# Expert stage of a transformer block: the three experts whose weights are loaded ahead become steps 0, 1 and 2, in place of steps 0, 2 and 4

## The reference, cut to what matters

```
p_grp = softmax(h @ wg + bg)            # 4 groups, the best one is taken
p_in  = softmax(le[token, grp])         # 8 experts in a group, the best 2 are taken
eidx  = grp * 8 + e_in                  # two experts per token
for each expert, over the rows (tokens) that chose it:
    hb = silu(xb @ w1[e]) * (xb @ w3[e])        # 1024 -> 512, twice
    y  = (hb @ w2[e]) * gate                     # 512 -> 1024
```

## Time and profile before

| | us |
|---|---|
| median of 3 runs | 1504.38 |
| the profiled execution | 1504.77 |
| its span | 1502.9 |
| TensorE busy in the span | 1333.3 (89%) |
| mean GB/s over the span | 214 |

### The profile page before, as it was taken

How to read it: one execution, slowest core, us unless ns; L and a number is a source line. 1 busy time by engine, 2 the same in 40 slices (tenths; PEclk the granted TensorE clock), 3 DMA queues, 4 the chain that set the end, 5 groups by cost and what they waited for, 6 DMA issues and landing times.

```text
span 1502.9 us, 17013 instructions
## 1 busy us (share of the span) xinstructions
PE 1333.3 (89%) x6325; PEld 672.8 (45%) x6325; DVE 596.4 (40%) x1331; ACT 396.5 (26%) x878; POOL 82.2 (5%) x113
## 2 busy tenths in 40 slices
PE   4899999999997889998899973999999999989940
PEld 3644444464665445544455541454344444434420
DVE  3526447510335766665522246232222322312216
ACT  4234311113666565554422220000000000000005
POOL 0000000010002100000000000000000000000014
PEclk9999999999998999999999985999999999999985
DMA  9712145330004692000092262899999999999979
GB/s 339 173 42 101 67 168 173 107 113 0 1 1 113 116 323 85 1 1 1 18 376 96 98 256 102 339 391 391 404 399 401 406 403 395 392 412 396 408 266 297
DMA packets 111534, 322.01 MB, mean 214 GB/s; under 512 B 28876, under 2 KB 53592, under 8 KB 103128
## 3 DMA queue, kind: packets, MB, share of 16 engines
q1 hardware_dynamic: 98376, 290.96, 52.5%
q0 software_dynamic: 6288, 18.90, 4.0%
q10 hardware_dynamic: 6784, 11.02, 2.0%
HBM read 280.44 MB, written 43.03 MB: 215 GB/s over the span
## 4 chain that ended last, share of the span: by engine, by line
PE 38%; DMA 8%; SPq 5%; DVE 4%; issue 2%; ACT 2%; POOL 1%; ACTq 0%; DVEq 0%; POOLq 0%
PE ps L1495 7%; PE ps L1550 7%; DMA arena<-expert_w 7%; PE ps L1539 7%; PE ps L1589 6%; SPq L675 4%; PE ps L1399 2%; PE ps L1416 2%; PE ps L1436 2%; PE ps L1529 1%; ACT arena L1064 1%; POOL arena L866 1%; PE ps L1470 1%; DMA arena<-d_y,arena 1%; SPq L673 1%
## 5 line engine op out<-in xcount | busy, mean ns | idle before, releaser
L1249 PE MATMUL ps<-arena 128*128 128x512 f32 x512 | 222.0, 593 | 0.0
L1550 PE MATMUL ps<-arena 128*32 128x256 f32 (+1 forms) x1408 | 189.7, 484 | 15.2 <-DMA arena<-expert_w 13.3
L1589 PE MATMUL ps<-arena 128*32 128x256 f32 (+2 forms) x832 | 152.7, 498 | 3.5 <-issue 2.2
L1249 PEld LDWEIGHTS ps<-arena 128*128 128x128 f32 x512 | 96.6, 190 | 117.8 <-issue 117.6
L1260 PE MATMUL ps<-arena 128*128 128x512 f32 (+1 forms) x384 | 144.5, 534 | 1.4 <-DVE arena L1685 1.4
L1550 PEld LDWEIGHTS ps<-arena 128*32 128x32 f32 (+1 forms) x1408 | 71.7, 123 | 118.8 <-issue 101.7
L1539 PE MATMUL ps<-arena 128*128 128x512 f32 x256 | 114.3, 604 | 2.8 <-DVE arena L2111 2.8
L1495 PE MATMUL ps<-arena 128*128 128x512 f32 x256 | 114.4, 599 | 0.0
L1064 ACT ACTIVATE arena<-arena 128x640 f32<-128x640 f32 (+7 forms) x128 | 92.7, 726 | 59.1 <-DVE arena L1899 59.1
L1260 PEld LDWEIGHTS ps<-arena 128*128 128x128 f32 x384 | 72.8, 192 | 66.2 <-issue 57.3
L1416 PE MATMUL ps<-arena 128*128 128x128 f32 x528 | 80.3, 286 | 24.2 <-ACT arena L1064 12.1
(11 more groups left out here) (339 smaller groups left out, 1267.7 us busy)
## 6 DMA issues: line engine op xcount, KB each, us to landing
arena<-expert_w SPq DMA_DIRECT2D x96, 2048.0 KB, 34.0
arena<-ada_w SPq DMA_DIRECT2D x12, 2048.0 KB, 9.3
d_y<-arena SPq DMA_DIRECT2D x25, 512.0 KB, 6.6
arena<-x SPq DMA_DIRECT2D x16, 512.0 KB, 5.2
arena<-w_in SPq DMA_DIRECT2D x4, 2048.0 KB, 10.8
d_y<-arena ACTq DMA_DIRECT2D x40, 128.0 KB, 7.9
arena<-w_out SPq DMA_DIRECT2D x2, 2048.0 KB, 14.1
out<-arena SPq DMA_DIRECT2D x8, 512.0 KB, 2.6
```

Source lines behind the costliest of these rows:

```text
L1249: last = nc.tensor.matmul(b, w(k), hT[:, k, 512 * c:512 * c + 512], start=(k == 0), stop=(k == KT - 1))
L1550: last = nc.tensor.matmul(ps[width * j:width * j + width, 2 if width == 64 else 3, 0:span], xgT[s][:, k, lo:lo + width], w_up[slots[n]][:, ...
L1589: last = nc.tensor.matmul(dst, hid_T[s][:, at_:at_ + width], w_down[slot][:, k, span * j:span * j + span], start=(k == 0), stop=(k == 3))
```

## The change

The first six entries of `ORDER` are put in another order. The places 0, 1 and 2 (128 rows each, weights loaded ahead) are steps 0, 1 and 2, and the places 27, 28 and 29 (32 rows each) are steps 3, 4 and 5. Steps 6 to 32 stay as they are.

```diff
-ORDER = [0, 27, 1, 28, 2, 29, 14, 7, 30, 15, 8, 16, 3, 32, 17, 9, 18, 19, 4, 10, 20, 21, 5, 11, 22, 23, 12, 6, 24, 25, 13, 26, 31]
+ORDER = [0, 1, 2, 27, 28, 29, 14, 7, 30, 15, 8, 16, 3, 32, 17, 9, 18, 19, 4, 10, 20, 21, 5, 11, 22, 23, 12, 6, 24, 25, 13, 26, 31]
```

## The result

The changed kernel took 1521.22 us (median of 4 runs, 1519.27 to 1521.90) against 1504.45: ratio 1.0111, 95% interval 1.0091 to 1.0130. It is slower, as forecast; 1516.4 with a range of 1510.5 to 1521.8 had been said. Measured again later, six runs of the same kernel had a median of 1516.12 against 1505.45 (ratio 1.0070, 1.0044 to 1.0096). The two intervals overlap but the medians differ by 5 us, and the reason for that is half of what there is to learn here.

A forecast was written before the change was run, and what follows sets the result against it. The prediction took the stream of weight loads to bound the expert stage. The profiled 1504.77 us plus 12.0 for its later opening gave 1516.8, less 0.4 to the median: 1516.4 us, range 1510.5 to 1521.8.

The forecast's parts named there:

- The bound: Expert stage: the weight-load stream, a queue not dry up to 1448 us, sets the end; TensorE follows it.
- The slots: Opening: slots come back later, loads 12, 14, 17 and 19 issued near 959, 974, 997 and 1002 us.
- The 12 us: Whole stream of weight loads and its last landing 12.0 us late, after two counts, 12.2 and 12.5.
- the opening's shortfall: 926 to 1000 us: 18.7 MB moved in place of 24.1, less 0.4 moved ahead; 5.0 MB short, 12.5 us.
- nowhere to catch up: Between 1005 and 1448 us the stream is full, so the opening's delay reaches the last landing undiminished.
- Rival D: Opening: isolated loads cheaper than counted, stores and gathers pass in gaps; 3.6 us less, 1512.8 us; chance 0.12.
- load 19: Opening: issued at 1002.0 us, landing at 1017.3 in place of 1005.1, so the stream is 12.2 us late.
- rival C: Steps 9, 10 and last down part: TensorE's clock low after waits, up to +5.3 us, 1521.7; chance 0.10.
- One sign: Near steps 9 and 10: TensorE's waits for weights sum to about 12 us more than the 3.52 before.
- The tail: Behind the last landing: same work, cost 0; moved read-back and result slots 0, at most 1 us either way.
- A: Whole kernel: TensorE is the bound and nothing moves but step 1's 0.9 us; 1505.3 us; chance 0.05.
- B: Expert stage: stream gets ahead during three 128-row steps, TensorE's waits and slow matmuls go; -16.3, 1488.1 us; chance 0.05.

The follow-up runs named there:

- late12: Kernel before, its step order kept, with load 12 and all loads behind it held until the first half of step 2 is done: 1518.13 us, ratio 1.0104.
- a_rows32: Changed kernel with steps 1 and 2 taking only 32 rows each, their other results left as zeros: 1500.29 us, ratio 0.9965.
- before_again: The kernel before, unchanged, run once more for a second profile of its end: profiled execution 1509.91 us, with the long stop.
- after_again: The changed kernel, unaltered, run six times more: 1511.70 to 1513.36 and 1518.88 to 1520.09 us in two groups, median 1516.12.
- b_noover: Kernel before without the loops, and so the jumps, over the unused overflow blocks on all engines: 1499.71 us, ratio 0.9975.
- b_oneif: Kernel before with one jump over the whole loop of unused overflow blocks in place of three: 1502.90 us, ratio 0.9981.
- half: Half of the reordering against the kernel before, steps 0 to 5 being places 0, 27, 1, 2, 28, 29: 1505.37 us, ratio 1.0013.
- a_noover: Changed kernel without the loops, and so the jumps, over the unused overflow blocks on all engines: 1511.80 us, ratio 1.0060.
- a_oneif: Changed kernel with one jump over the whole loop of unused overflow blocks in place of three: 1513.28 us, ratio 1.0056.
- a_x2late: Changed kernel with the 2 MiB residual read-back issued only after all engines joined behind the last step: 1514.44 to 1515.90 us, profiled run 1520.80.
- b_warm2: Kernel before with one jump over the unused blocks and 4 + 3 unused matmuls filling TensorE's idling before step 0: 1500.63 us, ratio 0.9964.

## Why the prediction was right, and where its size was off

**The bound.** Right. The stream of loads sets the end: late12 slowed the kernel by 1.04% with TensorE's order untouched, and a_rows32 took some 8 us of TensorE's work out of the opening alone and matched what the stream said, not what TensorE's time said.

**The slots.** Right. The times of TensorE's steps, worked out from rows of before, came within 1.9 us for each load, all on the early side, and 1.1 of it is that this execution's step 0 ended 1.1 us earlier.

**The 12 us.** Right in kind, and about 1 us too large. The times above are counted from the start of the span, and the expert stage does not begin at the same time in each execution: step 0's turning began at 927.15 in the first trace of before and at 926.39 in that of the changed kernel, at 928.73 in before_again and 927.01 in after_again. The stream's delay is cleaner within one execution: from the issue of load 10, which waits for step 0 alone in every order, to the landing of the last load. In before and in after_again the last load is this one (issue, and us to landing):

```profile
1410.73 10.26 SPq L673 DMA_DIRECT2D arena<-expert_w  x1
arena<-expert_w SPq DMA_DIRECT2D x1, 2048.0 KB, 37.6
```

```profile
1419.78 10.56 SPq L673 DMA_DIRECT2D arena<-expert_w  x1
arena<-expert_w SPq DMA_DIRECT2D x1, 2048.0 KB, 38.1
```

| order of steps | from load 10's issue to the last landing, us |
|---|---|
| of before (before, before_again, b_noover, b_oneif) | 506.9, 506.2, 506.5, 504.9 |
| half | 506.9 |
| new (after_again, a_noover, a_oneif, a_x2late) | 516.6, 517.4, 517.6, 517.2 |
| of before, load 12 held back (late12) | 517.2 |
| new, 32 rows in steps 1 and 2 (a_rows32) | 503.4 |

The new order makes the stream 11.1 us late between the means (9.7 to 12.7 between single profiles), where 12.0 had been summed, and late12 makes it as late with the old order. (The first trace of the changed kernel does not tell when its last load landed.) The term that was too large is the opening's shortfall. By bytes it was 24.1 - 19.5 = 4.6 MB, 11.5 us at 400 GB/s. The working had 24.1 - 18.7 = 5.4, less 0.4 for a gather moved ahead of 926 us; but from 900 to 926 us the changed kernel moved only 0.1 MB more than the one of before (79 and 76 GB/s).

"It has nowhere to catch up" holds, to within some 1 us. From 1000 to 1448 us the changed kernel did move 1.0 MB more (401 against 400 GB/s, then 407 against 394), but half of this is where the window ends: the queue of before is running out in it. What is left is little, and lies where TensorE waited: 430 GB/s from 1066.7 to 1076.2 us and 429 from 1082.5 to 1094.5 (why, no run shows). In the last 48 us before its own last down part the changed kernel moved 396:

```profile
1410.70:1458.70 48.00, 42.52 (x320) 18.40 (x316) 12.23 (x35) 1.82 (x4) 0.92 (x1) 0.96 0.98 396
```

Rival D had the right sign, but 3.6 us less than the forecast is too much. At load 19 alone the delay, counted from load 10, was 13.9 (77.5 against 63.7) and not 12.2. The sum for it left out what shares the engines with the last loads: from 995.00 to 1017.98 us 8.49 MB were moved, and three loads and two results are 7.3. The rest is the first part of load 20, and gathers; load 20's part is work done ahead and no loss of the stream, so the landing of one load is a poor measure of the whole.

**The slow clock, rival C.** It happened in part. The 32 matmuls at 1066.70 took 9.58 and the last 64-row down part 5.35 where it was 3.65; the latter made the end about 1 us later, since the last down part then waited for VectorE (0.72) and not for a load: in a_noover, which had it too, that part began at 1460.97 though the load had landed at 1459.8. In after_again the 64-row part took 3.65 and nothing was lost. So the cost is 0 to 1 us, not the 5.3 that C allowed. One sign that the prediction gave did not come: TensorE's waits for weights near steps 9 and 10 were to sum to about 12 more than 3.52, and they sum to 7.5 (0.29, 4.26 and 2.92), 4.0 more. TensorE was 9.9 us late all the same at the next 128-row up part (1113.63 against 1103.75): it also idled 2.85 before a down part at 1055.27 and lost 2.5 to the slow clock (9.58 for what took 7.10). The rule cited there, from the Trainium skill, "TensorE: Matmul & The Clock Gate", is borne out by the drop; it counts only where no queue covers it.

**The tail.** Costed at nothing but 1 us either way for moved slots, and that much was right for the program. What the sum left out is that the tail has two forms, and the one profile of before was of the short form. This is the term that the prediction put at nothing and that the first measurement contradicts. The 4.8 us between the forecast and that measurement (1516.4 and 1521.2) are 5 to 6 us for the long form, which all four first runs of the changed kernel seem to have had (the profiled one, which had it, is the lowest of them), less about 1 of the stream. That 1521.22 still fell inside the range is luck: its upper end, 1521.8, was there for C, which cost 0 to 1 us, and not for a second stop. The last down part and the first gather lie 10.1 us apart in the first trace of before and 9.1 in after_again, and 15.7 and 15.1 in the two with the long form. The net effect of the order itself is 7 to 12 us by five comparisons: 7.4, 9.4, 8.0 to 12.1, 10.4, and 10.7 for 1516.12 against 1505.45, where the groups are mixed. Pairs of single executions also carry the different starts of the stage: before_again began it 2.3 us later than the first trace of the changed kernel, so its 9.4 is rather too small.

**Rivals A and B.** A (1505.3) and B (1488.1) are out. B needed load 19 at 985.22 or earlier; it came at 1000.29.

What stays open: what decides whether an execution has the long stop. It isn't the order of the steps (before_again), nor the read-back beside it (a_x2late); late12 had it with the very TensorE program of before. That the runs of before also fall in these two forms is likely from their spread (1500.99 to 1510.30 in one batch), but it is seen in two profiles only.

## What to carry to other kernels

When a prefetch queue is full all the way to the end, the only place where the order of steps matters is where the queue is not yet full: count the bytes that the opening moves, and ask of each reordering when it gives buffers back, not how much ready work it puts first. Putting the steps that need no new data in a row looks like a head start for the transfers and is the opposite when each of them holds the buffers longest.

And before a difference of a few us is put down to a change, look at the tail of more than one profile: here an event that both programs have, worth some 6 us, was more than half as large as the effect itself. And measure a delay within one execution, from an event that the change cannot have moved: here the expert stage began up to 2.3 us earlier in one execution than in another, and that alone blurs a delay of 11 us.

## What the runs showed of the hardware that had not been expected

- A jump over code that is never executed can hold TensorE's sequencer for 3.4 to 5.1 us at the first pass (3.37 in late12, 5.13 in before), and in some executions 7.1 to 7.7 us more at the second (7.06 in late12, 7.72 in before_again); later passes take 0.2. The long form goes with more code fetches on the instruction queue (5 or 6 packets against 2 to 4). The Trainium skill, "Runtime: NRT & Kernel Launch", section "Instruction fetch mechanics", says that instructions come in blocks of 16 KiB by the sequencer's own DMA, that the fetch runs ahead only in sequence, and that a taken branch to code outside the two blocks at hand has to wait for a fetch. The traces agree in kind. They add that three passes over the same jump cost differently from one execution to the next, which the page doesn't say.
- Filling 6.6 and 2.8 us of idling with 5.8 and 2.7 us of unused matmuls (b_warm2) brought the granted clock of the opening from 0.93 to 1.00 and a 128-row up part from 16.22 to 14.00 us.
